# Latent attention: the multiplication that makes the probabilities of the first tile of tokens moved from VectorE to GpSimd, with a semaphore of its own

## What is computed

```
s     = einsum('bqhc,bqkc->bqhk', q_full, keys) * C_SCALE
pr    = softmax(where(valid, s, -inf), axis=-1)
o_lat = einsum('bqhk,bqkc->bqhc', pr, values)
o     = einsum('bqhc,chd->bqhd', o_lat, w_uv)
```

## Time and profile before

| what | us |
|---|---|
| median of 3 runs | 2233.03 |
| lowest and highest run | 2232.91, 2234.67 |
| the profiled execution, its own time | 2237.57 |
| its span | 2235.8 |
| TensorE busy in the span | 1823.7 |
| VectorE busy in the span | 959.7 |
| ScalarE busy in the span | 798.3 |
| GpSimd busy in the span | 178.7 |
| latent attention, first scores to the last values | 1967.96 to 2000.43 |

### The profile page before, as it was taken

One profiled execution on the slowest core, in us unless ns is written; L12 is line 12 of the kernel. 1 busy time (PEld: TensorE's weight loads), 2 busy tenths in 40 slices (PEclk: granted clock), 3 DMA queues, 4 the chain that ended last, 5 costly groups with the idle time before them and its releaser, 6 DMA issues.

```text
span 2235.8 us, 26767 instructions
## 1 busy us (share of the span) xinstructions
PE 1823.7 (82%) x10682; PEld 1160.8 (52%) x10682; DVE 959.7 (43%) x1677; ACT 798.3 (36%) x1422; POOL 178.7 (8%) x183
## 2 busy tenths in 40 slices
PE   7998999999986665655565656556999999889999
PEld 5875788789941111111111111113857888768887
DVE  5687787866640000000000000002757747777745
ACT  5654577675320000000000000003855536566533
POOL 0200221262020000000000000000000000420000
PEclk9999999999998778787878787888999999999999
DMA  8644243446799999999999999998524564325562
GB/s 328 226 185 159 87 132 123 137 134 237 263 372 428 427 429 428 428 429 428 428 429 428 429 429 428 428 428 336 209 78 163 187 234 149 131 92 174 184 235 95
DMA packets 68310, 618.93 MB, mean 277 GB/s; under 512 B 8288, under 2 KB 17248, under 8 KB 22768
## 3 DMA queue, kind: packets, MB, share of 16 engines
q1 hardware_dynamic: 56464, 598.70, 66.9%
q10 hardware_dynamic: 9392, 10.63, 1.9%
q0 software_dynamic: 2352, 8.19, 1.1%
HBM read 616.39 MB, written 1.11 MB: 276 GB/s over the span
## 4 chain that ended last, share of the span: by engine, by line
PE 53%; DMA 37%; DVE 5%; ACT 3%; issue 1%; POOL 0%; SPq 0%; DVEq 0%; ACTq 0%; POOLq 0%
DMA ring<-in_w_edown 18%; DMA ring<-in_w_eup 17%; PE bank L542 10%; PE bank L543 9%; PE bank L544 9%; PE bank L2974 5%; PE bank L2976 3%; PE bank L2766 2%; PE bank L2783 2%; PE bank L3414 1%; PE bank L1911 1%; DMA ring<-in_w_ada 1%; PE bank L1344 1%; ACT ring_parts L504 1%; PE bank L1252 1%
## 5 line engine op out<-in xcount | busy, mean ns | idle before, releaser
L2870 DVE TENSOR_TENSOR work<-bank,work 128x512 f32<-128x512 f32 x14 | 9.7, 691 | 803.0 <-PE bank L2766 803.0
L510 DVE TENSOR_TENSOR ring_parts<-ring,ring_parts 128x2048 fp32r<-128x2048 f32 (+2 forms) x125 | 280.7, 2251 | 154.1 <-ACT ring_parts L504 153.6
L504 ACT CAST ring_parts<-ring 128x2048 fp32r<-128x2048 f32 (+3 forms) x151 | 276.4, 1835 | 177.3 <-DMA ring<-in_w_mlp_out 81.5
L2766 PE MATMUL bank<-ring,work 128*32 128x512 f32 x1008 | 169.7, 808 | 128.3 <-DMA ring<-in_w_egate 66.5
L2783 PE MATMUL bank<-ring,work 128*32 128x512 f32 x1020 | 176.5, 826 | 103.1 <-DMA ring<-in_w_edown 97.7
L2766 PE MATMUL bank<-work 128*32 128x512 f32 x1040 | 150.8, 710 | 93.7 <-DMA work<-in_w_eup 66.5
L542 PE MATMUL bank<-hT_hi,ring_parts 128*128 128x256 f32 (+2 forms) x584 | 195.3, 334 | 0.8 <-ACT work L1179 0.4
L544 PE MATMUL bank<-hT_hi,ring_parts 128*128 128x256 f32 (+2 forms) x584 | 187.1, 320 | 0.0
L543 PE MATMUL bank<-hT_lo,ring_parts 128*128 128x256 f32 (+2 forms) x584 | 186.9, 320 | 0.0
L2974 PE MATMUL bank<-hn_parts,ring_parts 128*128 128x512 f32 x512 | 181.6, 400 | 0.0
L2766 PEld LDWEIGHTS bank<-ring,work 128*32 128x32 f32 x1008 | 33.6, 130 | 258.0 <-issue 107.6
(11 more groups left out here) (482 smaller groups left out, 3560.8 us busy)
## 6 DMA issues: line engine op xcount, KB each, us to landing
ring<-in_w_edown SPq DMA_DIRECT2D x62, 2048.0 KB, 26.2
work<-in_w_eup SPq DMA_DIRECT2D x33, 2048.0 KB, 26.8
work<-in_w_egate SPq DMA_DIRECT2D x32, 2048.0 KB, 26.1
ring<-in_w_egate SPq DMA_DIRECT2D x32, 2048.0 KB, 26.0
ring<-in_w_eup SPq DMA_DIRECT2D x31, 2048.0 KB, 25.9
ring<-in_w_mlp_in SPq DMA_DIRECT2D x32, 1024.0 KB, 4.8
ring<-in_w_mlp_out SPq DMA_DIRECT2D x30, 1024.0 KB, 4.8
ring<-in_w_ada SPq DMA_DIRECT2D x12, 2048.0 KB, 10.1
```

What stands on the lines that cost most here:

```text
L504: act.copy(halves_of(name, ring_parts)[1], halves_of(name, ring)[0]).then_inc(hi_made, 1)
L510: dve.tensor_tensor(lo, halves_of(name, ring)[0], hi, ALU.subtract).then_inc(lo_made, 1)
L2766: last = pe.matmul(bank[which][32 * n:32 * n + 32, :], rows[:, 2 * c + k2, :], w[:, k2, 512 * n:512 * n + 512], start=c == 0 and k2 == 0, ...
```

## The change

Three pieces of code change. The wait for probabilities becomes a method, `wait_probs`, which for `AC` asks a new semaphore `lead_probs` for units of the first tile and the old `att_probs` for units of the second. In `att_dve`, where `by_pool` says that a pair of units belongs to GpSimd, VectorE takes the reciprocal, raises the new semaphore `lead_shares` and goes on, without a wait for its own instruction and without the two multiplications. GpSimd gets a new function at the end of `c_pool` that waits for `lead_shares`, and makes the two multiplications of the first tile of each block.

```diff
+            def wait_probs(self, eng, u):
+                eng.wait_ge(att_probs, self.first + u + 1)
+
+            by_pool = staticmethod(lambda u: False)
...
-                    pe.wait_ge(att_probs, A.first + u + 1)
+                    A.wait_probs(pe, u)
...
-                    dve.wait_ge(att_probs, A.first + (i - SOFT) // A.parts + 1)
+                    A.wait_probs(dve, (i - SOFT) // A.parts)
...
-                    link(dve.reciprocal(stat[:, SHARE, pair], stat[:, TOTAL, pair]))
...
-                    probs(i)
-                    probs(i + 1)
+                    share = dve.reciprocal(stat[:, SHARE, pair], stat[:, TOTAL, pair])
+                    if A.by_pool(i):
+                        share.then_inc(lead_shares, 1)
+                    else:
+                        link(share)
...
+                        probs(i)
+                        probs(i + 1)
...
+        AC.by_pool = lambda u: unit(u)[1] == 0
+
+        def wait_latent_probs(eng, u):
+
+            blk, qt, side = unit(u)
+            if qt == 0:
+                eng.wait_ge(lead_probs, 2 * blk + side + 1)
+            else:
+                eng.wait_ge(att_probs, AC.first + 2 * blk + side + 1)
+        AC.wait_probs = wait_latent_probs
+
+        def lead_probs_pool(pool):
+
+            for blk in range(C_HEADS // 2):
+                pool.wait_ge(lead_shares, blk + 1)
+                for side in range(2):
+                    u = 4 * blk + side
+                    if u >= AHEAD:
+                        pool.wait_ge(att_turned, AC.first + u - AHEAD + 1)
+                    pool.tensor_scalar(AC.pr[:, u % AHEAD, 0:P], AC.s(u)[:, 0:P], stat[:, SHARE, u % SOFT:u % SOFT + 1], None,
+                                       ALU.mult).then_inc(lead_probs, 1)
+
...
+            lead_probs_pool(pool)
```

More of the change, by code:

```diff
@@ L1205, in build @@
         stat = sb("stat", [P, 3, SOFT])
+        lead_shares, lead_probs = sem("lead_shares"), sem("lead_probs")
         LEAST, TOTAL, SHARE = range(3)
@@ L1290, in att_dve @@
                     dve.wait_ge(att_exp, A.sets + i + 2)
-                    link(dve.reciprocal(stat[:, SHARE, pair], stat[:, TOTAL, pair]))
-                    if A.parts == 2:
-                        second = stat[:, SHARE, i % SOFT + 1:i % SOFT + 2]
-                        link(dve.tensor_tensor(second, second, lam_of[0], ALU.mult))
-                    probs(i)
-                    probs(i + 1)
+                    share = dve.reciprocal(stat[:, SHARE, pair], stat[:, TOTAL, pair])
[3 more added lines that the diff above has]
+                        link(share)
+                        if A.parts == 2:
+                            second = stat[:, SHARE, i % SOFT + 1:i % SOFT + 2]
+                            link(dve.tensor_tensor(second, second, lam_of[0], ALU.mult))
+                        probs(i)
+                        probs(i + 1)
                 for i in (step - TURN - 4, step - TURN - 3):
```

## The result

| | before | changed |
|---|---|---|
| median of 16 runs each, us | 2233.69 (2229.50 to 2237.94) | 2236.66 (2234.38 to 2242.68) |
| ratio to before, 95% interval | | 1.0015 (1.0009 to 1.0022) |
| profiled execution: own time, span, us | 2237.57, 2235.8 | 2237.80, 2236.0 |
| latent attention, first scores to last values, us | 1967.96 to 2000.43: 32.47 | 1963.80 to 2000.78: 36.98 |
| period of a steady block, us | 3.74 | 4.01 |

The change costs 3.4 us (2.0 to 4.9), still within 0.2%, but 3 us more than predicted and above the range, which ended at 2236.0. The two profiled executions differ by 0.2 us only, because the changed one reached the stage 4.2 us earlier. From the last values to the end of the span they take 235.3 and 235.2 us. So what the change did is read from the stage.

A forecast was written before the change was run, and what follows sets the result against it. No engine is full; a loop of waits bounds the latent attention, ScalarE's path ending last. A late first transpose adds 0.4 us, freed VectorE time 0: 2233.03 + 0.4 = 2233.4 us, range 2232.0 to 2236.0.

The forecast's parts named there:

- The bound: Latent attention block: a loop of waits sets the 3.74 us period; of VectorE's and ScalarE's paths, ScalarE's ends last.
- The slack: First transpose of a block can come 0.12 to 0.20 us later at no cost; starting it earlier brings nothing.
- VectorE's freed time worth 0: Two multiplications, 0.48 us a block, removed from VectorE turn into its idle time; value 0.
- The hand-overs: Path to the first transpose: reciprocal to GpSimd 0.09 us, GpSimd's product to TensorE 0.05 to 0.06.
- The product, D = 0.40: GpSimd's 128x128 multiplication by a column, priced at 0.40 us from a two-tensor multiplication; first transpose 0.17 us later.
- The sum: 0 to 0.25 us in blocks 2 to 6, 0.34 in the first two, last 0: 0.34 to 0.59, taken as +0.4.
- Rival 1: Slower by a slow product: at 0.608 us, 1.7 to 2.1 us more, 2235.1; chance 0.10 for D 0.45 to 0.99, 0.03 above.
- The last block at 0: Last block: no scores follow and the values wait for a copy over 0.4 us behind the transpose; cost 0.
- The second product is covered: GpSimd's second product of a block ends at 1982.06, before its transpose at 1982.95, covered by the values.
- Rival 2: GpSimd's first product is slow: 1.5 us gives 2234.9; chance 0.03 for 1 to 4.5 us, 0.04 for more.
- Contention at 0: VectorE's copy and bias beside GpSimd's new products, reading PSUM, do not slow; cost 0.
- Signs given in advance: Wrong if period grows 0.2 or more, values ignore the copy, first product is long or late, or narrow bias exceeds 0.29.

The follow-up runs named there:

- early share: Changed kernel, share of the two narrow units taken before the wide units' bias, from the second block on: blocks 3.74 us, ratio 1.0001.
- Copy first: Kernel before, ScalarE copying a block's first wide unit's turned probabilities ahead of the next block's first wide exp: blocks 3.63 us, ratio 0.9996.
- two-tensor product: Changed kernel, GpSimd's product written as a multiplication of two tensors, the column read by a stride of zero: blocks 3.79 us, ratio 1.0002.
- copy moved: Kernel before, copy of each block's last wide unit's turned probabilities moved from ScalarE to VectorE: blocks 3.97 us, ratio 1.0003.
- second product only: Changed kernel, with VectorE making each block's first product and GpSimd only the second: blocks 3.74 us, ratio 1.0002.
- 12-run repeat: Changed kernel measured again, nothing altered, 12 runs: stage 34.72 us, blocks 4.01 us, ratio 1.0016.
- early share with late values: Changed kernel, narrow units' share taken early and a block's values issued one step later on TensorE: blocks 3.85 us, ratio 1.0004.
- changed with copy first: Changed kernel, ScalarE copying a block's first wide unit's turned probabilities ahead of the next block's first wide exp: blocks 4.01 us, ratio 1.0018.

## Why the prediction was wrong, step by step

- **The bound** (two paths, of which ScalarE's holds the values): right. The early share, which takes VectorE's and GpSimd's part away, did not shorten the block at all, and in that kernel TensorE waits for ScalarE's copies. Copy first, which shortens ScalarE's path alone, took 0.11.
- **The slack**, 0.12 to 0.20: it is 0.10 to 0.11, by the two-tensor product and the changed kernel (lateness less growth), by copy moved (3.74 less 3.63), and by the start of the values (0.60 less 0.49). A little under the lower end. The first value matmul follows the last score after 0.20 us (1985.47 to 1985.67), which was the longer of the two steps that the bounds came from; the shorter one, 0.12, does not hold here.
- **VectorE's freed time worth 0**: right, by the kernel with the second product only.
- **The hand-overs**, 0.09 and 0.06: right. 1984.43 to 1984.52, and 1985.13 to 1985.18.
- **The product, D = 0.40: this is the step that failed.** It measured 0.605, the top of the range that the step gave (0.608, a single slow one of 32). The row that I took had the same engine, size and type, but another form of instruction, and "same operation" was wrong: a multiplication of two tensors and one by a column are two instructions. The two-tensor kernel had 0.398 and with it the predicted blocks, 3.79 us. A product of 0.605 in place of 0.40 costs 1.6 us of the stage (34.72 less 33.12), more than half of the 3.0 by which the forecast was short. It does not alone put the time out of the range: by the prediction's own price a product of 0.608 gives 2235.1. The rest is the clock, the first block and the base, since before's median of 16 runs lies 0.66 us above the one of three that the forecast started from. The Trainium skill (GPSIMD Engine Reference, 4.1 Engine selection) has GpSimd about equal to VectorE with one input. The measurement decides against it for this form: 0.605 us against VectorE's 0.28, and slower than the two-input form.
- **The sum.** Rival 1 was priced at just this D: 1.7 to 2.1 us, at a chance of 0.10. Measured, where the clock stays up (the 12-run repeat against before): first transpose +0.38, block 0 to 1 +0.50, block 1 to 2 +0.38, five steady blocks 5 x 0.265 = +1.32, and the last block gives back 0.33. That is 2.25 us. By the prediction's own steps with the measured numbers it would be 7 x 0.375 less 5 x 0.11 of slack, 2.08, and 0.12 to 0.14 more in the first block (the next point but one): 2.2.
- **The last block at 0**: right. The lateness that had been built up at its transpose, 2.58 us, is 2.25 at its end.
- **"The second product is covered"**: right in the steady blocks, wrong in the first. No values lie between its two transposes, and the second follows after 0.59 us in place of 0.40. I had checked the cover in a steady block only. But this is not what makes the first block cost 0.50 and not 0.38, for the two-tensor kernel has the same extra 0.13 without that wait. It comes by VectorE's first narrow bias, 0.44 us behind the transpose in place of 0.09, for a reason that stays open.
- **The clock**: missing, a term put at nothing. I read a granted clock of 1.00 for before and carried it over. With the fall the stage is 4.5 us longer (4.7 with the starts counted alike), without it 2.25. If half of the executions had it, the mean would be 3.5 us; if 7 in 20, as many as profiles with the late start, 3.1. The measured difference is 3.4 (2.0 to 4.9), but how often the clock falls in unprofiled runs no record shows, so this is an agreement and not a proof.
- **Rival 2** (a slow first product): fell. 0.605 like the others, started 0.10 us behind its releaser.
- **Contention at 0**: right, the bias beside a product keeps 0.28 to 0.29.
- **Signs given in advance.** "The period grows by 0.2 or more" and "the values start without regard to the copy" both came true; by my own list I was wrong there. The change "within 0.2%" held.

What stays open is what brings the clock down. It fell in 3 of 6 profiles of kernels that have a product of 0.605 us on the path of the first block and no filler (changed, one repeat of it, early share; not in the other repeat, early share with late values, changed with copy first), and in 0 of 13 profiles of kernels in which the first block's product was on VectorE alone, or took 0.40, or only the second was GpSimd's. That ties it to the slow product in the first block, and within the six the fall came with the 0.34 us start and never with the other. It does not say which pause it is, and the one attempt to fill a pause had the start with which no fall was seen at all.

## What to carry to other kernels

A price taken from a row holds for that form of instruction: the same multiplication on the same engine cost 0.40 or 0.61 us by the form alone. If two paths end within 0.11 us of each other, a shorter one of them gains at most that, and what an edit adds to one costs all but that; here only edits to both, with copies put in another order, freed TensorE. Cover has to be looked for in the first block of a loop too, where the work that covers later on doesn't exist yet, and a pause added there can cost clock.

## What the runs showed of the hardware

- GpSimd's multiplication by a column (TENSOR_SCALAR, 128x128, f32) takes 0.592 to 0.607 us in the changed kernel, and the last of the stage 0.718; the two-tensor form with the column read by a stride of zero takes 0.396 to 0.401. VectorE's multiplication by a column takes 0.283.
- The granted clock of TensorE can fall to a half for 6.83 us (or 3.41, in the kernel with the early share) in one execution of a program and not in the next. It fell after the shorter pause, 1.45 us, and not after the longer, 1.61; with the idle time ahead of the scores both come to 1.79.
- 6.83 us at 1.2 GHz made the stage 2.4 us longer (33.76 against 31.33 from the first transpose on; 36.98 against 34.72 with starts that differ by 0.16).
